# Expert rows by indirect DMA from DRAM, three weight buffers and a new order on TensorE, in a two-layer encoder with hierarchical experts

## What is computed

```python
def hier_moe(h, w_rg, b_rg, w_re, b_re, w_g, w_u, w_d):
    t = h.reshape(T, D)                       # h = RMSNorm(x) * g
    gidx = argmax(t @ w_rg + b_rg)            # one group of 4
    gw = softmax(t @ w_rg + b_rg)[gidx]
    elog = (t @ w_re + b_re)[group gidx]      # its 8 experts
    top_v, top_i = top_k(elog, 2)
    top_w = softmax(top_v) * gw
    ...
    a, u = t @ w_g[e], t @ w_u[e]             # 1024 -> 256, for 32 experts
    y = sum over the token's two experts of (silu(a) * u * top_w) @ w_d[e]
```

## Time and profile before

| | |
|---|---|
| median of the runs | 1479.92 us |
| profiled execution, its span | 1482.5 us |
| PE busy in the span | 1347.2 us (91%) |
| DVE, ACT, POOL busy | 618.3, 459.5, 222.4 us |
| DMA, mean over the span | 199 GB/s; 294.99 MB |

### The profile page before, as it was taken

One profiled execution on the slowest core, in us unless ns is written; L12 is line 12 of the kernel. 1 busy time (PEld: TensorE's weight loads), 2 busy tenths in 40 slices (PEclk: granted clock), 3 DMA queues, 4 the chain that ended last, 5 costly groups with the idle time before them and its releaser, 6 DMA issues.

```text
span 1482.5 us, 20481 instructions
## 1 busy us (share of the span) xinstructions
PE 1347.2 (91%) x7048; PEld 913.0 (62%) x7049; DVE 618.3 (42%) x1404; ACT 459.5 (31%) x815; POOL 222.4 (15%) x153
## 2 busy tenths in 40 slices
PE   6999988999989999999499999689999899999991
PEld 5877766788855444445287777478888545444440
DVE  3567775333362222222355767742333622222214
ACT  5434344433231212111243344433333211111113
POOL 0323220121120000000012323102220200000000
PEclk9999999999999999999799999999999999999996
DMA  5322210543515999998333323025335089999964
GB/s 188 118 84 94 89 54 15 213 170 99 206 65 210 387 383 374 381 387 353 149 102 100 98 81 93 22 86 209 131 112 229 1 345 380 379 383 384 380 235 190
DMA packets 51629, 294.99 MB, mean 199 GB/s; under 512 B 8400, under 2 KB 8400, under 8 KB 36192
## 3 DMA queue, kind: packets, MB, share of 16 engines
q1 hardware_dynamic: 45888, 281.57, 51.2%
q0 software_dynamic: 5520, 11.70, 2.1%
q10 hardware_dynamic: 144, 0.76, 0.1%
HBM read 274.60 MB, written 18.87 MB: 198 GB/s over the span
## 4 chain that ended last, share of the span: by engine, by line
issue 49%; PE 34%; POOL 8%; DVE 4%; DMA 3%; ACT 1%; POOLq 0%; DVEq 0%; SPq 0%; ACTq 0%
PE bank L690 13%; PE bank L703 8%; PE bank L678 7%; POOL qk_b L1420 3%; POOL mab L1426 2%; DMA y_rows<-yb,idx_row 2%; PE bank L684 2%; PE bank L669 2%; DVE xg L1288 2%; POOL m_lo L1428 1%; POOL qk_a L1415 1%; DMA yld<-y_rows 1%; ACT m_hi L901 1%; DVE yb L1031 0%; POOL h_lo L1436 0%
## 5 line engine op out<-in xcount | busy, mean ns | idle before, releaser
L426 PE MATMUL bank<-h_hi,w_hi 128*128 128x512 f32 x640 | 254.1, 397 | 6.6 <-DVE h_lo L1048 3.6
L428 PE MATMUL bank<-h_hi,w_lo 128*128 128x512 f32 x640 | 250.2, 391 | 0.0
L427 PE MATMUL bank<-h_lo,w_hi 128*128 128x512 f32 x640 | 249.7, 390 | 0.0
L690 PE MATMUL bank<-gu,xgt 128*64 128x512 f32 x1024 | 225.3, 592 | 0.5 <-issue 0.5
L1006 DVE TENSOR_TENSOR w_lo<-raw,w_hi 128x1024 fp32r<-128x1024 f32 x112 | 142.2, 1270 | 186.5 <-ACT w_hi L784 185.6
L690 PEld LDWEIGHTS bank<-gu,xgt 128*64 128x64 f32 x1024 | 74.2, 137 | 146.4 <-issue 146.4
L784 ACT ACTIVATE w_hi<-raw 128x1024 fp32r<-128x1024 f32 x112 | 118.1, 1055 | 101.0 <-PE bank L428 101.0
L426 PEld LDWEIGHTS bank<-h_hi,w_hi 128*128 128x128 f32 x640 | 120.5, 188 | 32.9 <-DVE h_lo L1048 4.0
L428 PEld LDWEIGHTS bank<-h_hi,w_lo 128*128 128x128 f32 x640 | 120.5, 188 | 25.9
L427 PEld LDWEIGHTS bank<-h_lo,w_hi 128*128 128x128 f32 x640 | 120.7, 189 | 23.8
L703 PE MATMUL bank<-dn,zt 128*64 128x512 f32 x512 | 116.9, 598 | 0.9 <-ACT zt L952 0.9
(11 more groups left out here) (192 smaller groups left out, 1865.4 us busy)
## 6 DMA issues: line engine op xcount, KB each, us to landing
gu<-in_gu_w SPq DMA_DIRECT2D x30, 4096.0 KB, 13.7
dn<-in_dn_w SPq DMA_DIRECT2D x30, 2048.0 KB, 10.2
raw<-in_stream SPq DMA_DIRECT2D x112, 512.0 KB, 3.3
swp<-pj SPq DMA_DIRECT2D x136, 64.0 KB, 2.0
gu<-in_gu_w SPq DMA_DIRECT2D x16, 512.0 KB, 4.4
yld<-y_rows SPq DMA_DIRECT2D x16, 512.0 KB, 7.4
dn<-in_dn_w SPq DMA_DIRECT2D x8, 512.0 KB, 4.2
x<-in_x SPq DMA_DIRECT2D x4, 512.0 KB, 6.5
```

The lines of the kernel that those rows point to most:

```text
L426: mm(dst, ah, bh, start=start, stop=False)
L427: mm(dst, ah, bl, start=False, stop=False)
L428: return mm(dst, al, bh, start=False, stop=stop)
L690: last = mm(bank[4][e * CAP:(e + 1) * CAP, :], xgt[:, k, e * CAP:(e + 1) * CAP], gu[s][:, e, k, :], start=k == 0, stop=k == KD - 1)
```

## The change

- `h2_tile` makes x times its rms factor only (the norm's weight vector is applied later), in three buffers, and POOL stores the four tiles to a DRAM tensor `h2_rows`. `h2_hi`, `h2_lo` and the loads of `g_row` in the layers are gone. The fourth tile waits until the first store has landed (`h2_st0`).
- `info` holds row numbers only. `read_info` takes 4 matmuls, and `slots` writes one number for the row to read (`idx_h`) and one for the row to write (`idx_y`), for each pair in a column of its own.
- POOL fetches the pair's rows with an indirect DMA from `h2_rows` to `xg`, one buffer. `gather_rows` and the copies to `xg` are gone.
- After the transposes DVE alone copies both halves to `xgt`, with the norm's weights, into one of two buffers. Up products have two banks.
- `yb` is copied without a scale and has one buffer; the weights enter when `yld` is added to x.
- Three buffers for the weights (`RING`). Pair 0 and pair 1 come in pieces, pair 1 between tiles of the output projection; pair 2 is issued when that projection is done; pair p waits for pair p-3.
- The loops over the pairs are written out in Python.

Below, the parts of SP, of PE, of DVE, of POOL and of the combine, in this order.

```diff
+    gu = [at(f"gu{i}", r, [2, KD, 2 * FE], FP32) for i, r in enumerate((R_W, R_H, R_Q))]
+                    if NQ + NGATE + 2 <= i < NQ + NGATE + 6:
+                        for n in range(3):
+                            load_piece(l, 1, 3 * (i - NQ - NGATE - 2) + n)
+                sp.wait_ge(w_used, (l + 1) * NT)
+                for p in range(2, PAIRS):
+                    if p >= RING:
+                        sp.wait_ge(gu_ok, l * PAIRS + p - RING + 1)
+                    load_gu(l, p)
+                    if p >= RING:
+                        sp.wait_ge(dn_ok, l * PAIRS + p - RING + 1)
+                    load_dn(l, p)
...
+                where(0)
+                where(1)
+                keep_busy(bank[6][:, :], 4)
+                rows_in(0)
+                for n in range(PAIRS):
+                    pe.wait_ge(xtd_ok, n0 + n + 1)
+                    landed(first_gu, gu_ld, n)
+                    up(n % 2, n % 2, n % RING, gu_ok)
+                    if n + 1 < PAIRS:
+                        rows_in(n + 1)
+                    if n:
+                        down_pair(n - 1)
+                    pe.wait_ge(z_ok, n0 + n + 1)
+                    turn_z(zt_ok)
+                    if n + 2 < PAIRS:
+                        where(n + 2)           # wait sel_ok, ix_ok, then read_info
+                down_pair(PAIRS - 1)
...
+                def turned(s, done):
+                    for kh in range(2):
+                        k4 = slice(4 * kh, 4 * kh + 4)
+                        last = tt(xgt[:, s, k4, :], bank[2 + kh][:, :].rearrange("p (k n) -> p k n", k=4),
+                                  g2_col[:, k4].rearrange("p (k o) -> p k o", o=1).to_broadcast([P, 4, P]), ALU.mult)
+                    last.then_inc(done, 1)
+                for n in range(PAIRS):
+                    if n + 2 < PAIRS:
+                        choose(n % 2, 2 * (n + 2), sel_ok)
+                    dve.wait_ge(sil_ok, n0 + n + 1)
+                    tt(z[:, :], bank[n % 2][:, FE:2 * FE], sil[:, :], ALU.mult).then_inc(z_ok, 1)
+                    if n + 1 < PAIRS:
+                        dve.wait_ge(xgt_ok, n0 + n + 2)
+                        turned((n + 1) % 2, xtd_ok)
+                    if n:
+                        y_half(n - 1)
+                    if n + 2 < PAIRS:
+                        dve.wait_ge(inf_ok, n0 + n + 3)
+                        slots(n + 2, ix_ok)
...
+                for t in range(TT):
+                    hold(pool, h2_ok, l * TT + t + 1)
+                    pool.dma_start(h2_rows[t * P:(t + 1) * P, :], xn2[t % 3][:, :]).then_inc(h2_st0 if t == 0 else h2_st, 16)
...
+                for n in range(PAIRS):
+                    if n:
+                        pool.wait_ge(xgt_ok, n0 + n)
+                    hold(pool, ix_ok, n0 + n + 1)
+                    gather(n, xg_ld)
+                    if n >= 2:
+                        pool.wait_ge(ya_ok, n0 + n - 1)
+                        hold(pool, yd_ok, n0 + n - 1)
+                        scatter(n - 2, ysc)
...
-                    tt(x[:, t, :], x[:, t, :], yld[:, 0, t, :], ALU.add)
+                    stt(x[:, t, :], yld[:, 0, t, :], wts[:, t, 6:7], x[:, t, :], ALU.mult, ALU.add)
```

More of the change, by code:

```diff
@@ L29 @@
 PAIRS = NE // 2
-BIG = 4096.0
 NEVER = 1000.0
 NLOG = NGRP + NE
+RING = 3
+MORE_AT = {s: sum(1 for n in range(2, PAIRS) if n % RING == s) for s in range(RING)}
 PARAMS = KD * NLOG + NLOG + 2 * KD + 8
@@ L659, in _, with read_info @@
                 keep_busy(bank[7][:, :], 2)
[L662 to L666, removed]
+                def read_info(s, e0, done):
                     for t in range(TT):
-                        last = mm(bank[5][:, 2 * P:2 * P + 4], sel[:, s, t, :].bitcast(FP32), info[:, t, :, bass.ds(e0, 2)],
+                        last = mm(bank[7][:, 0:4], sel[:, s, t, :], info[:, t, :, bass.ds(e0, 2)],
                                   start=t == 0, stop=t == TT - 1)
-                    last.then_inc(info_done, 1)
-                def gather_rows(s, done):
-                    for t in range(TT):
-                        for half in range(2):
-                            for n, part in enumerate((h2_hi, h2_lo)):
-                                last = mm(bank[half][:, :], sel[:, s, t, :], part[:, t, half * T:(half + 1) * T],
-                                          start=t == 0 and n == 0, stop=t == TT - 1 and n == 1)
                     last.then_inc(done, 1)
@@ L744, in _, with landed @@
-                with pe.Fori(0, PAIRS // 2 - 1) as it:
-                    pair(it, 0)
-                    pair(it, 1)
-                pair(PAIRS // 2 - 1, 0)
-                pair(PAIRS // 2 - 1, 1, True)
+                def landed(first, later, n):
+                    if n < 2:
+                        pe.wait_ge(first[n], (l + 1) * (8 if first is first_gu else 4) * 16)
+                    else:
+                        nth = sum(1 for p in range(2, n) if p % RING == n % RING)
+                        pe.wait_ge(later[n % RING], (l * MORE_AT[n % RING] + nth + 1) * 16)
@@ L773, in _ @@
             act.dma_start(cst[:, :], consts).then_inc(cst_ld, 16)
[L774 to L775 removed]
+            act.sem_inc(hi_ok, ahead[hi_ok])
             act.sem_inc(sig_ok, ahead[sig_ok] + 2)
@@ L1442, in _ @@
-                with pool.Fori(0, PAIRS // 2) as it:
-                    for s in range(2):
-                        n = l * PAIRS + it * 2 + s
-                        need(pool, ya_ok, n + 1)
-                        hold(pool, yd_ok, n + 1 + ahead[yd_ok])
-                        scatter(s, ysc[s])
+                    hold(pool, h2_ok, l * TT + t + 1)
+                    pool.dma_start(h2_rows[t * P:(t + 1) * P, :], xn2[t % 3][:, :]).then_inc(h2_st0 if t == 0 else h2_st, 16)
+                n0 = l * PAIRS
@@ L1449, in more_experts @@
+                for n in range(PAIRS - 2, PAIRS):
+                    pool.wait_ge(ya_ok, n0 + n + 1)
+                    hold(pool, yd_ok, n0 + n + 1)
+                    scatter(n, ysc)
                 def more_experts(r, p, q):
+                    hold(pool, ov_ix, q + 1)
+                    gather(0, ov_ga)
                     hold(pool, ov_y, q + 1)
```

325 lines of the change are left out of this document (124 added, 201 removed).

## The result

| | before | after |
|---|---|---|
| median of the runs | 1479.92 us | 1651.45 us (1643.57 to 1653.32) |
| ratio to before on the same chip | | 1.1137, 95% interval 1.1113 to 1.1161 |
| profiled execution, its span | 1482.5 us | 1649.8 us |
| PE busy in the span | 1347.2 us (91%) | 1272.6 us (77%) |
| DMA, mean | 199 GB/s | 186 GB/s |

What follows compares the result with a forecast made beforehand. PE bounds the kernel before; after the change a loop through POOL would, at 1.7 + 12.2 + 4.7 + 0.9 = 19.5 us a pair. Each layer ends 21.3 us later: 1479.92 + 2 x 21.3 = 1522.5 us, range 1425 to 1575.

Steps and rivals of the forecast that it cites:

- L: On POOL's queue, from the scatter's issue to the gather's landing: 12.2 us, between 9.6 and 16.8.
- the lower clock in turn and down: PE's clock may fall after idling, making turn and down up to 4.6 us longer; 0.9 us taken.
- down(0) + 13 P + 15.6: Layer's last down ends 13 pair periods and 15.6 us after down(0), at 744.0 for a period of 19.5.
- PE's own work: On PE, turn, down, up, turn_z and half of read_info together take 12.5 us a pair.
- the stream's period: On the DMA engines, weights plus scatter and gather need about 16.1 us a pair.
- the DMA share: Sign in the profile after: the DMA engines' busy share should fall to 0.8.
- the period of 19.5 us: Loop from down through scatter, gather, turn to the next down: 18.6 us plus 0.9 for the clock.
- The opening: Layer's start: up(0) starts at about 451.4, bounds 449 and 456, and down(0) ends at 474.9.
- Rival 1: Gather lands in time, L 9.6 or less; weights' stream sets 16.1 us a pair: 1434 us, chance 0.34.
- Rival 2: PE's idle time brings 1.2 GHz for all of turn and down in every pair: 1587 us, chance 0.09.
- Rival 4: Third buffer and early loads don't do what they say, or opening costs more: a few us; no separate chance.
- the forecast case: Loop through POOL sets a pair's period, from 17.9 to 21.5 us: 1480 to 1574 us, chance 0.52.

Runs made afterwards that it cites:

- the small write: Changed kernel with the scatter of pairs 8 to 14 a plain write of 8 pieces of 512 B, pairs 0 to 7 of all rows: 1613.35 us.
- the swapped order: Changed kernel with POOL issuing the gather of pair n+1 ahead of the scatter of pair n-2: 1532.61 us, ratio 1.0349 to the kernel before.
- the version with both edits: Changed kernel with POOL's gather(n+1) ahead of scatter(n-2), and row numbers and slots of pair n+2 made ahead of turn(n+1): 1437.06 us.
- SP's order mended: The version with both edits, with SP issuing gate and up weights of pair p+1 ahead of down weights of pair p: 1422.76 us.

## Why the prediction was right and wrong

The direction and the mechanism held, and the size was off by more than the range allowed: 1651.45 us against 1522.5 and at most 1575. Two terms of the loop were priced too low: the rows' way behind the scatter (L), and the lower clock in turn and down.

**What held.** PE waits at turn for the DMA into `xg`, in 14 of 14 pairs of the stretch. Scatter and gather stand together right behind each down (1.43 us apart, for 1.15). The way from down's end to the scatter is 1.8 us, for 1.7. Up(0) starts at 451.7, for 451.4. The way from down(13) to the end of the layer's last down is 15.5 us, for 15.6. The relation "down(0) + 13 P + 15.6" gives 480.7 + 13 x 24.14 + 15.6 = 810.1, and the trace has 810.0. Without the weights' stream, with down(0) at 474.2 and P 12.34, it gives 650.2, and that trace has 650.1. PE's own work is 12.3 us a pair, for 12.5, and the stream's period 16.4, for 16.1. Two of the signs named beforehand came out stronger than stated, as the size did: the waits are 9.3 us on average, for 4 to 7, and the DMA share is 0.70, for 0.8.

**The step that failed: the period of 19.5 us.** The mean over 13 periods is 24.14 in the first layer (24.7 over the first twelve, then 16.8) and 23.56 in the second.

| term of the period | predicted | measured (one pair) |
|---|---|---|
| down's end to the scatter's issue | 1.7 | 1.8 |
| L, to the landing | 12.2 | 15.7 |
| PE's wake | 0.2 | 0.2 |
| turn and down, with the clock | 4.5 + 0.9 | 6.3 |
| sum | 19.5 | 24.0 |

*L, +3.5 us.* The bounds of 9.6 and 16.8 held it. What failed is the choice between them, "the scatter's landing and one more data part of about 4". The scatter lands in 9.6 us (median), for 8.4, and the data part behind it takes 6.1 us, for about 4. I had that 4 from the 4.3 us in which a scatter's 144 packets ran. That price takes no account of the size of the weights' packets beside them. The first line below has those of the earlier trace rows, 9.7 KB each on average; the second those beside the gather's packets in the changed kernel, from 588.6 to 594.7 us, 16.4 KB each:

```profile
q1 hardware_dynamic: 119, 1.16, 76.3%
...
q1 hardware_dynamic: 152, 2.49, 95.2%
```

By the packet counts above the rows' packets go one by one between them. One number stays open: with the scatter's packets all but gone L is still 12.2, the value that I had taken for both.

*The clock, +0.9 us.* The idle time before turn is 9.9 us, not 6, and in it the granted clock falls from 1.00 in up to 0.50 (windows of the changed kernel, up and then the middle of the wait). Each of the first layer's downs up to down(13) takes 4.2 to 5.8 us, for 3.65 at the full clock:

```profile
554.00:561.00 7.00, 7.00 (x34) 2.28 (x33) 1.55 (x9) 0.46 (x2) 2.13 (x2) 1.00 0.89 329
...
565.00:568.00 3.00, 0.00 (x0) 0.00 (x0) 0.00 (x0) 0.00 (x0) 0.00 (x0) 0.50 1.08 457
```
The half clock does not last all of turn and down, though, so the term is 1.8 and not 4.6. It does not come from the longer L: turn and down take 6.3 us after the wait of 9.9 us, 6.4 after 6.1 us (the small write, turn at 709.15), and 7.1 and 6.1 after 6.0 and 4.2 us (the swapped order, turns at 571.39 and 590.40). So it was too low at the forecast's own wait of 6 us as well. The run with the small write shows the two apart: at an L of 12.2, just the forecast's, the period is 20.3 us and not 19.5.

**The sum.** Against 19.5 the periods cost 13 x 4.64 + 13 x 4.06 = 113.1 us in the two layers. The opening adds 5.8 (0.3 of it in the start of up(0)) and 3.1: up(0) to down(0)'s end is 29.0 and 26.6 us where 23.5 was forecast, with gather(2) landing in 10.7 us in place of 8.4 and down(0) at the lower clock. The second layer's up(0) comes 1.9 us later after the first's last down than before, where 1.35 earlier was forecast: 3.3. Together 125.3 us; the span is 1649.8 and the forecast one 1482.5 + 42.6 = 1525.1, 124.7 apart.

**The rivals.** Rival 1, that the gather lands in time, did not hold in the changed kernel, but it describes the version with both edits well: "The end is 699.8" (697.5 there), 1434 us (1437.06), and "down to 1420" with the head start (1422.76 with SP's order mended). Its threshold of 11.5 us for L left the clock out: in small packets L was 11.1, for which the loop gives 17.5 us at the full clock, but turn and down took 6.9 us (584.57 to 591.47) in place of 4.5, the mean period was 19.5 and the time 1529. Rival 2, the clock that feeds itself, was right that it falls in every pair, and its 22 us a period is the nearest of the cases. In part that is luck: it had a clock term of up to 4.6 and no longer L, and the period got there by a term of 1.8 and an L of 15.7. I gave it 0.09, on one row for and one against it. The sentence on the Trainium skill's formula (DMA: Bandwidth & Descriptors, section Anatomy of one DMA), by estimate 2.6 us for these rows, stands beside 4.0 us without the weights' stream and 14.5 with it. The measurements decide. Rival 4 holds in that the third buffer cured no wait, with 8 us a layer at the last pair that I had not counted.

**The range.** Both ends of L stood in the text, but the range did not use them. Its 1575 is the forecast case at a period of 21.5, which with the clock term of 0.9 is an L of 14.2. With L at 16.8 the period is 24.1, the layer's end 803.8 and the time 1642 us; with the clock term that was measured, 1.8, it is 25.0, the layer's end 474.9 + 13 x 25.0 + 15.6 = 815.5 and the time about 1665 us. A range that takes in the bounds of the unknown costs, as it should, would have reached there.

## What to carry to other kernels

An indirect DMA of 128 rows beside a stream of large packets was a latency of 10 to 15 us here, against 4 without the stream. Price it by its number of packets and by the time of the packets beside which they run, not by its bytes. Ask what its issue waits for and what stands ahead of it in its engine's program and in its queue, and issue it as soon as its own inputs are there, ahead of any operation that waits for something later. Where PE, the DMA engines and the clock are all below full in the same slices, look for the loop, write its terms down, and change the order. Here a buffer more was worth 16 us and an input that came earlier nothing until the order was right, and 47 and 96 us after. Where a term of a loop is known only between two bounds, carry both bounds through to the range.

## What the runs showed of the hardware

- A gather of up to 128 rows of 4 KB landed in 4.0 us with little beside it, 9.8 under the weights' stream when issued first, 11.4 behind an all but empty write, and 14.5 behind a scatter. With the stream in 4 KB packets the last was 9.7.
- While both queues had work, they moved packets in nearly equal numbers: 49 and 51 from 587 to 589 us in the changed kernel with weights' packets of 16 KB, 147 and 140 from 579 to 581 us with packets of 3.7 KB.
- Two indirect DMAs of one queue, issued 1.3 to 1.4 us apart, kept their order: whichever came first landed in 9.6 to 9.8 us under the stream of 16 and 8 KB packets and the other in 14.5 to 15.0 us from its own issue.
- The granted clock fell to 1.2 GHz after an idle time of PE of 2.3 us, when turn had already begun; in the stretch of the earlier trace rows an idle time of 2.89 us had left it at 2.4 GHz. What tells the two apart was not tested.
- POOL's indirect DMA instruction took 1.0 to 1.1 us of its engine, for gather and scatter alike.
